# On VectorE, the sums of a vector panel put ahead of the split of the next weight panel

## The chip, the cores and the metric

The kernel runs on one core of one Trainium2 chip, as one launch. The metric is device time in microseconds. A core has TensorE (PE in the rows; its weight loads are PEld), VectorE (DVE), ScalarE (ACT), GpSimd (POOL) and SyncE (SP, which here only issues DMAs). Each engine works through its own instructions in order and waits on semaphores for the others.

## The reference, cut to what matters

Two blocks of two layers each are evaluated on 256 latent and 256 context tokens of width 1024, all in float32. The first block is a mixer (low-rank attention and neighbourhood attention behind gates) with an MLP, twice; the second is an mLSTM layer and a windowed attention layer. Every layer begins with a modulated norm whose shift, scale and gate come from a condition vector:

```
mod = silu(c) @ w_ada[layer] + b_ada[layer]          # (1024) @ (1024, 6 * 1024)
shift, scale, gate, ... = split(mod)                 # the vectors
x = x + gate * f(norm(x) * (1 + scale) + shift)
f: h @ w_in, gates, attention, w_out; relu(h @ w_ff1)**2 @ w_ff2
```

`c` is one vector for the latent tokens and another for the context tokens. So there are matrix products with 512 tokens, and matrix-vector products with one or two columns, and both read large weights from HBM.

## The kernel before, in words

All weights are read as 261 panels of at most 128 x 2048 floats (1 MB), in one list `items` that `plan()` writes. SyncE issues them in exactly that order into three buffers `raw[0..2]`, panel i into `raw[i % 3]`; it waits before each until panel i - 3 has been consumed. There are two kinds.

A weight panel is a 256-column piece of a matrix (8 chunks of 128 rows). To multiply in float32 accuracy it is split: ScalarE rounds it to `whi` (`hi`, L1236, two instructions of half a panel), VectorE subtracts to get the rest, `wlo` (`lo`, L1829, two halves). Then `raw` is free. `whi` and `wlo` have two buffers each, so `hi` of a panel also waits until TensorE is done with the panel two before it. TensorE multiplies hi x hi, hi x lo and lo x hi: 2 x 8 x 3 = 48 matmuls of 512 columns for a panel (L579 to L581 in `weight_left`), half of them for panels of 4 chunks (`mo`, `no`), and half the columns in layer 1, where only latent tokens count. It may start when the first half of `lo` is there (`weights`) and needs the other in mid panel (`rest`).

A vector panel ("ada") is 256 rows of a modulation matrix, 1024 columns. The first eight are multiplied on TensorE; the other 64 go to VectorE. `beside(p)` takes the vector panel that follows weight panel p in the list (the table `WITH`, built from `AFTER`) and adds c[k] * w[k] into `parts_of[0]` (latent) and `parts_of[1]` (context): four instructions of 128 x 1024 (L1824, in a vector's first panel two of them L1819), or two where only the latent part is needed (`LATENT_ONLY`). Four panels make one vector, q = 0 to 3. At q = 1 `beside` first reads the finished row of the vector before (`rows_out`). After the fourth, TensorE adds the partial sums up over the 128 partitions (`vector_sums`, L707), at the end of its panel p: there it waits for the sums (`("parts", r)`). ScalarE then copies the row (L1255) and TensorE turns it (L718) at the end of the next panel.

On VectorE the order is written by hand. `begin(p)` makes the `lo` of the weight panel after p, while TensorE works on p; `beside(p)` follows it; then comes what p's product needs: in the head loop (L2174 on) the branches of `mo` and `no`, in `wo` and `ff2` the residual and, in places, the sums of squares, in `ff1` the squared relu, in `mo` and `mz` of the mLSTM the output gates. Sixteen vectors ride this way: four in the head loop and `wo` of layer 0 (q = 3 falls on gm1, gn2, no3 and ff1's third panel), seven in the MLP of layer 0 (three of them full, r 7, 9 and 11, three for the latent part alone, and the one ahead of the turn to the next norm, full), one in `gn` of layer 1, one in `mq`, one in `mk`, two in `mo`.

```
def begin(p):                      # VectorE
    lo_to(next_weight(p))
# SyncE, per panel p of the list, q = items[p.i - 3]
wait used(q) if q is a vector panel else lo(q, 1);  dma_start(raw[p.slot], p)
```

Of the kernel before, what the change touches and what calls it, by code (L numbers as in the profile page):

```python
# [298 lines left out]
def program(nc, d, out):  # L299
    with ExitStack() as ctx:  # L300
# [131 lines left out]
        def S(n):  # L432
            return small[:, SMALL[n][0]:SMALL[n][1]]
# [6 lines left out]
        at = {p.key: p for p in items}  # L440
# [1366 lines left out]
        def vector(e):  # L1807
# [6 lines left out]
            def tt(o, a, b, op, *names):  # L1814
                e.tensor_tensor(o, a, b, op).then_inc(*up(ve, *names))  # L1815
# [7 lines left out]
            def stt(o, a, s_, b, o1, o2, *names):  # L1823
                e.scalar_tensor_tensor(o, a, s_, b, o1, o2).then_inc(*up(ve, *names))  # L1824
# [16 lines left out]
            def begin(p):  # L1841
                lo_to(next_weight(p))
# [204 lines left out]
            def first_layer(l):  # L2047
# [44 lines left out]
                for n, a in (("q", 1), ("k", 1)):  # L2092
                    p = at["na", l, 2 * "qk".index(n) + a]
                    begin(p)
                    beside(p)
                    tl = tiles if n == "q" else [0, 1, 2, 3]
                    if n == "k":
                        begin(at["uq", l, 0])
                    for tile in tl:
                        e.wait_ge(*done(("nsq", l, n, tile)))  # L2100
                        e.tensor_reduce(nss[n][:, 0, tile], work[:, tile, :].rearrange("p (h e) -> p h e", e=64), AX.X,
                                        ALU.add).then_inc(*up(ve, ("nsum", l, n, tile)))
                    if n == "q":
                        begin(at["na", l, 2])
                        beside(at["na", l, 2])
                    r = slice(tl[0], 4)
                    rsqrt_fine(nss[n][:, 1, r], nss[n][:, 0, r], nss[n][:, 2, r], 64, ("ns", l, n), ("nrt", l, n))
                    if n == "k":
                        begin(at["uq", l, 1])
                    for tile in tl:  # L2110
                        v = ntok(n, tile).rearrange("p c (h e) -> p c h e", e=64)
                        g_ = nss[n][:, 1, tile].rearrange("p (c h) -> p c h", h=2).unsqueeze(3).to_broadcast([128, 4, 2, 64])
                        tt(v, v, g_, ALU.mult, ("na normed", l, n, tile))
# [39 lines left out]
                a = tiles[0]  # L2153
                rsqrt_fine(mrms[:, 1], msums[:, 1], mscr[:, :, :], 96, ("ms", l, "k"), ("mrt", l, "k"))
                for tile in range(4):
                    w = ktok[:, tile]
                    tt(w, w, mrms[:, 1, tile].unsqueeze(2).to_broadcast([128, 8, 96]), ALU.mult, ("k normed", l, tile))
                rsqrt_fine(mrms[:, 0, a:4], msums[:, 0, a:4], mscr[:, a:4], 96, ("ms", l, "q"), ("mrt", l, "q"))
                begin(at["na", l, 4])
                beside(at["na", l, 4])  # L2160
                for n, dst in (("q", mqT), ("k", mkT)):
                    first = q0 if n == "q" else 0
                    for h in range(1, 8, 2):
# [9 lines left out]

                for h in range(4):  # L2174
                    for kind in ("gm", "gn", "mo"):
                        if h or kind != "gm":
                            begin(at[kind, l, h])
                        beside(at[kind, l, h])
                    for j in range(2):
                        key, u = ("mo", l, h, j), utmp[j][:, 0:nq]  # L2180
                        e.wait_ge(*done(("full", key)))
                        e.wait_ge(*done(("sig", l, "gm", h, j)))
                        tt(u, banks(key)[:, 0:nq], u, ALU.mult, ("read", key))
                    begin(at["no", l, h])
                    beside(at["no", l, h])
                    for j in range(2):
                        c = 2 * h + j
                        key, u = ("no", l, h, j), utmp2[j][:, 0:nq]
                        e.wait_ge(*done(("full", key)))
                        e.wait_ge(*done(("sig", l, "gn", h, j)))  # L2190
                        tt(u, banks(key)[:, 0:nq], u, ALU.mult, ("read", key))
                        own()
                        tt(u, u, utmp[j][:, 0:nq], ALU.add, ("ymix", l, c))
                        e.wait_ge(*done(("yhi", l, c)))
                        own()
                        tt(gYl[:, c, q0:T], u, gYh[:, c, q0:T].bitcast(F32), ALU.subtract, ("ylo", l, c))
# [7 lines left out]
                    return key if last else (*key, x)  # L2204

                for a in range(3):
                    begin(at["wo", l, a])
                    beside(at["wo", l, a])
                    for j in range(2):
                        residual(s, 2 * a + j, ("wo", l, 2 * a + j), "b", l, 2, parts)  # L2210
                        stat(s, 2 * a + j, parts)
# [7 lines left out]
                m = n = 0  # L2219
                for kind, g in MLP_ORDER:  # L2220
                    for a in range(4):
                        begin(at[f"ff{kind}", l, 4 * g + (1 if (kind, g, a, l) == (1, 0, 0, 0) else a)])
                        if kind == 2 and g == 3 and a == 3:
                            rows_out()
                            if not last:
                                fold("b", 1, 1, "gattn1")
                            turn(after, *(("s", 0, 1, 0) if last else ("b", 1, 1, 0)), parts,
                                 lambda j, x: residual(after, 6 + j, split_key(("ff2", l, 3, 6 + j), x), "b", l, 5, x),
                                 at["mq", 1] if last else at["ckv", 1, 1])
                            continue  # L2230
                        beside(at[f"ff{kind}", l, 4 * g + a])
                        for j in range(2):
                            c = 2 * a + j
                            if kind == 1:
                                u, v = utmp[m % 2][:, q0:T], utmp2[m % 2][:, q0:T]
                                e.wait_ge(*done(("relu", l, m)))
                                tt(v, u, u, ALU.mult, ("hsq", l, m))
                                e.wait_ge(*done(("hhi", l, m)))
                                own()
                                tt(H[g % 2][1][:, c, q0:T], v, H[g % 2][0][:, c, q0:T].bitcast(F32), ALU.subtract, ("hlo", l, g, c))  # L2240
                                m += 1
                            else:
                                residual(after, c, ("ff2", l, g, c), "b", l, 5, parts)
                                if g == 3:
                                    stat(after, c, parts)

                        if last:
                            if n == 1:
                                rows_out()
                                fold("s", 0, 1, "gnorm0")  # L2250
                            if n < 8:
                                stat("s0", n, "c")
                            elif n == EARLY:
                                rms("s0", "c")
                            elif n <= EARLY + 8:
                                scaled("s0", n - EARLY - 1, "c", "s", 0, 1)
                                left("s0", n - EARLY - 1, "c", "s", 0, 0)
                        n += 1

            def lstm_layer():  # L2260
# [10 lines left out]
                for o, m in ((tri[0], zb), (tri[1], zf)):  # L2271
                    ts(o[:, :], m[:, 384:512], -1.0, None, ALU.is_ge, None)
                for a in range(4):
                    if a:
                        begin(at["mq", a])
                    beside(at["mq", a])
                begin(at["mg", 0])
                key = ("mgT",)
                e.wait_ge(*done(("full", key)))
# [12 lines left out]
                for dr, order in ((0, (0, 1, 2, 3)), (1, (1, 0, 3, 2))):  # L2292
                    e.memset(pre[:, dr, order[0]], 0.0).then_inc(*up(ve))
                    for before, tile in zip(order, order[1:]):
                        own()
                        tt(pre[:, dr, tile], pre[:, dr, before], lf[:, before, dr, :], ALU.add, "gate pre")
                for a in range(4):
                    begin(at["mk", a])
                    beside(at["mk", a])
                    if a == 0:  # L2300
                        key = ("gsum",)
                        e.wait_ge(*done(("full", key)))
# [78 lines left out]
                mark(ve, "lstm dve end")  # L2381
                for g in range(2):
                    for a in range(4):
                        begin(at["mo", 4 * g + a])
                        beside(at["mo", 4 * g + a])
                        for j in range(2):
                            c = 8 * g + 2 * a + j
                            e.wait_ge(*done(("lsig", c)))
                            own()
                            stt(hnT[:, c, :], hnT[:, c, :], S("mlhg")[:, c:c + 1], s1[j][:, :], ALU.mult, ALU.mult)  # L2390
                        begin(at["mz", 4 * g + a])
                        beside(at["mz", 4 * g + a])
                        for j in range(2):
                            c = 8 * g + 2 * a + j
                            u = s1[2 + j][:, :]
# [226 lines left out]
```

## Time and profile before

| what | us |
|---|---|
| median of 3 runs | 2124.77 (2123.84 to 2125.97) |
| profiled execution | 2125.6 |
| its span, first to last instruction | 2123.8 |
| TensorE busy | 2002.0 (94%) |
| VectorE busy | 1374.1 (65%) |
| ScalarE busy | 908.7 (43%) |
| mean granted clock of TensorE | 0.976 |

The span is what the trace holds; the profiled execution's own time is 1.8 us more. Busy time is the time in which an engine has at least one instruction at work. The granted clock is 1.0 at TensorE's full rate of 2.4 GHz and 0.5 at 1.2 GHz.

### The profile page before, as it was taken

What the parts mean: (1) busy time and instruction counts of PE and PEld (TensorE: products, weight loads), DVE (VectorE), ACT (ScalarE), POOL (GpSimd) and SP (SyncE); (2) the same over time, 40 slices, a digit from 0 to 9 for tenths busy, and PEclk for the clock granted to TensorE, in tenths of its full rate; (3) what the DMA queues carried; (4) which work ended last, traced back from release to release, by engine and by line L of the source; (5) the groups of instructions that cost most, each with busy time, mean ns of one, the idle gap of its engine ahead of it and who ended that gap; (6) DMA issues with size and microseconds to landing.
All of it is one profiled execution on the core that took longest, in us unless ns stands there. A gap on an engine that the chain in (4) does not pass through costs nothing. (4 is left out here: it accounts for less than half of the span.)

```text
span 2123.8 us, 30218 instructions
## 1 busy us (share of the span) xinstructions
PE 2002.0 (94%) x12098; PEld 1674.8 (79%) x12098; DVE 1374.1 (65%) x2452; ACT 908.7 (43%) x1632; POOL 58.3 (3%) x83
## 2 busy tenths in 40 slices
PE   5999998988999999899999899998999999999998
PEld 3888776768787777698779899996787778888877
DVE  4447765668676766775676677665466665464886
ACT  4346752224422232255574465433243433233685
POOL 0000000001000000010000000000000000000100
PEclk9999999999999999999999899999999999999999
DMA  8222015443345454434107455534311133332311
GB/s 298 95 90 95 16 41 198 159 158 120 139 160 197 159 198 159 154 134 144 46 27 274 161 189 181 187 137 167 139 61 40 41 119 144 114 140 102 135 61 41
DMA packets 47099, 277.05 MB, mean 130 GB/s; under 512 B 4464, under 2 KB 12784, under 8 KB 16880
## 3 DMA queue, kind: packets, MB, share of 16 engines
q1 hardware_dynamic: 42080, 266.94, 34.1%
q10 hardware_dynamic: 4736, 7.34, 1.1%
q8 instruction: 96, 1.57, 0.3%
q0 software_dynamic: 144, 0.85, 0.1%
q14 instruction: 43, 0.35, 0.0%
HBM read 273.01 MB, written 2.10 MB: 130 GB/s over the span
## 5 line engine op out<-in xcount | busy, mean ns | idle before, releaser
L579 PE MATMUL ps<-t 128*128 128x512 f32 (+1 forms) x2176 | 761.8, 350 | 12.7 <-DVE t L1829 11.0
L580 PE MATMUL ps<-t 128*128 128x512 f32 (+1 forms) x2176 | 752.8, 346 | 0.0
L581 PE MATMUL ps<-t 128*128 128x512 f32 (+1 forms) x2176 | 752.5, 346 | 0.0
L1829 DVE TENSOR_TENSOR t<-t 128x1024 fp32r<-128x1024 f32 (+2 forms) x372 | 417.0, 1161 | 269.8 <-ACT t L1236 268.9
L1236 ACT ACTIVATE t<-t 128x1024 fp32r<-128x1024 f32 (+2 forms) x378 | 360.0, 1000 | 304.6 <-DMA t<-in_panels 188.7
L579 PEld LDWEIGHTS ps<-t 128*128 128x128 f32 x2176 | 416.3, 191 | 77.3 <-DVE t L1829 14.6
L580 PEld LDWEIGHTS ps<-t 128*128 128x128 f32 x2176 | 416.3, 191 | 50.7 <-issue 0.7
L581 PEld LDWEIGHTS ps<-t 128*128 128x128 f32 x2176 | 415.4, 191 | 51.5
L1824 DVE SCALAR_TENSOR_TENSOR t<-t 128x1024 f32<-128x1024 f32 (+7 forms) x415 | 332.6, 838 | 27.1 <-ACT t L1336 14.1
L1815 DVE TENSOR_TENSOR t<-t 128x512 f32<-128x512 f32 (+10 forms) x621 | 228.9, 389 | 154.1 <-ACT t L1273 41.7
L1336 ACT ACTIVATE t<-ps 128x512 f32<-128x512 f32 (+1 forms) x244 | 114.8, 491 | 244.0 <-PE ps L581 130.4
L660 PE MATMUL ps<-t 128*128 128x256 f32 (+1 forms) x524 | 158.9, 303 | 0.4 <-DVE t L1829 0.2
L662 PE MATMUL ps<-t 128*128 128x256 f32 (+1 forms) x524 | 152.2, 291 | 0.0
L661 PE MATMUL ps<-t 128*128 128x256 f32 (+1 forms) x524 | 152.2, 290 | 0.0
L1824 DVE SCALAR_TENSOR_TENSOR t<-ps,t 128x256 f32<-128x256 f32 (+2 forms) x176 | 83.2, 496 | 83.0 <-PE ps L581 59.2
L660 PEld LDWEIGHTS ps<-t 128*128 128x128 f32 x524 | 100.7, 192 | 9.4 <-issue 3.0
L661 PEld LDWEIGHTS ps<-t 128*128 128x128 f32 x524 | 100.8, 192 | 3.7 <-issue 2.2
L662 PEld LDWEIGHTS ps<-t 128*128 128x128 f32 x524 | 100.6, 192 | 1.4
L1815 DVE TENSOR_TENSOR t<-ps,t 128x128 fp32r<-128x128 f32 (+5 forms) x134 | 52.2, 394 | 63.1 <-ACT t L1704 31.5
L1359 ACT ACTIVATE t<-ps,t 128x512 f32<-128x512 f32 (+1 forms) x128 | 87.0, 696 | 10.2 <-DVE t L1815 10.2
L1273 ACT ACTIVATE t<-t 128x256 f32<-128x256 f32 (+1 forms) x62 | 30.9, 503 | 129.8 <-DVE t L1824 114.5
L1819 DVE TENSOR_SCALAR t<-t 128x512 f32<-128x512 f32 (+5 forms) x182 | 79.4, 477 | 2.5
(171 smaller groups left out, 2055.6 us busy)
## 6 DMA issues: line engine op xcount, KB each, us to landing
t<-in_panels SPq DMA_DIRECT2D x235, 1024.0 KB, 4.9
t<-in_panels SPq DMA_DIRECT2D x18, 512.0 KB, 4.0
t<-in_panels SPq DMA_DIRECT2D x8, 768.0 KB, 4.1
t<-in_window ACTq DMA_DIRECT2D x4, 768.0 KB, 4.3
t<-in_ctxT SPq DMA_DIRECT2D x1, 1024.0 KB, 13.4
t<-in_xT SPq DMA_DIRECT2D x1, 1024.0 KB, 15.5
t<-in_ctxT ACTq DMA_DIRECT2D x1, 1024.0 KB, 5.7
t<-in_xT ACTq DMA_DIRECT2D x1, 1024.0 KB, 5.6
```

The lines of the kernel that those rows point to most:

```text
L579: e.matmul(o, hi[:, k, w], xh[:, c0:c1], start=k == 0, stop=False)
L580: e.matmul(o, hi[:, k, w], xl[:, c0:c1], start=False, stop=False)
L581: t = e.matmul(o, lo[:, k, w], xh[:, c0:c1], start=False, stop=k == p.nk - 1)
L660: e.matmul(o, xh[:, r], hi[:, k, n0:n1], start=k == 0, stop=False)
L661: e.matmul(o, xh[:, r], lo[:, k, n0:n1], start=False, stop=False)
L662: t = e.matmul(o, xl[:, r], hi[:, k, n0:n1], start=False, stop=k == p.nk - 1)
L1236: e.activation(p.half(whi[p.buf], a), p.half(raw[p.slot], a), ACT.Copy).then_inc(*up(se, ("hi", p.i, a)))
L1336: e.activation(o, i, func, scale=scale).then_inc(*up(se, ("read", key), *names))
L1359: e.activation(work[:, 2 * par + g, x * w:x * w + w], banks(("s", s, i, g))[:, x * w:x * w + w], ACT.Exp, scale=sc_, bias=nm[:, c:c + 1], ...
L1815: e.tensor_tensor(o, a, b, op).then_inc(*up(ve, *names))
L1824: e.scalar_tensor_tensor(o, a, s_, b, o1, o2).then_inc(*up(ve, *names))
L1829: e.tensor_tensor(p.half(wlo[p.buf], a), p.half(raw[p.slot], a), p.half(whi[p.buf], a).bitcast(F32), ALU.subtract).then_inc(*up(ve, ("lo", ...
```

## The change

On VectorE `beside(p)` is called ahead of `begin(p)` in place of behind it, wherever both stand together. TensorE's, ScalarE's and SyncE's programs are the same text. In the MLP the call also moves ahead of the branch for the last panel, which has no vector panel. `beside` of the `na` and `mz` panels returns at once, as no vector panel follows them.

```diff
@@ the head loop of the first block
                 for h in range(4):
                     for kind in ("gm", "gn", "mo"):
+                        beside(at[kind, l, h])
                         if h or kind != "gm":
                             begin(at[kind, l, h])
-                        beside(at[kind, l, h])
...
+                    beside(at["no", l, h])
                     begin(at["no", l, h])
-                    beside(at["no", l, h])
...
                 for a in range(3):
+                    beside(at["wo", l, a])
                     begin(at["wo", l, a])
-                    beside(at["wo", l, a])
...
@@ the MLP
                     for a in range(4):
+                        beside(at[f"ff{kind}", l, 4 * g + a])
                         begin(at[f"ff{kind}", l, 4 * g + (1 if (kind, g, a, l) == (1, 0, 0, 0) else a)])
...
-                        beside(at[f"ff{kind}", l, 4 * g + a])
@@ the mLSTM layer
                 for a in range(4):
+                    beside(at["mq", a])
                     if a:
                         begin(at["mq", a])
-                    beside(at["mq", a])
...
                 for a in range(4):
+                    beside(at["mk", a])
                     begin(at["mk", a])
-                    beside(at["mk", a])
...
+                        beside(at["mo", 4 * g + a])
                         begin(at["mo", 4 * g + a])
-                        beside(at["mo", 4 * g + a])
...
+                        beside(at["mz", 4 * g + a])
                         begin(at["mz", 4 * g + a])
-                        beside(at["mz", 4 * g + a])
```

The same exchange stands at `na` 2 and `na` 4.

## Rows read from the trace of the kernel before

**Rows 1.** The waits of the whole span: engine, line, waited for: us, times, longest.
```profile
PE ps L707 <- DVE t L1824: 50.9, 10, 8.1
PE ps L579 <- DVE t L1829: 11.0, 12, 2.5
...
DVE t L1829 <- ACT t L1236: 268.9, 147, 15.1
...
ACT t L1236 <- DMA t<-in_panels: 188.7, 45, 11.2
...
ACT t L1236 <- PE ps L581: 76.1, 14, 9.5
```
**Rows 2.** TensorE's waits in stretches: 330-460, 540-560, 600-860, 885-900, 1110-1165, 1440-1530.
```profile
PE ps L707 <- DVE t L1824: 21.2, 3, 8.1
...
PE ps L707 <- DVE t L1824: 4.3, 1, 4.3
...
PE ps L707 <- DVE t L1824: 10.7, 3, 3.9
...
PE ps L707 <- DVE t L1824: 5.1, 1, 5.1
PE ps L718 <- ACT t L1255: 2.6, 1, 2.6
...
PE ps L579 <- DVE t L1829: 4.0, 6, 1.6
...
PE ps L707 <- DVE t L1824: 9.6, 2, 6.0
```
**Rows 3.** Timeline of the MLP: start, duration, engine, line, operation, [idle before <-releaser].
```profile
641.73 2.36 DVE L1829 TENSOR_TENSOR t<-t 128x1024 fp32r<-128x1024 f32 x2 [3.90 <-ACT t L1236]
644.00 4.87 DVE L1824 SCALAR_TENSOR_TENSOR t<-t 128x1024 f32<-128x1024 f32 x4
648.98 1.85 DVE L1824 SCALAR_TENSOR_TENSOR t<-ps,t 128x256 f32<-128x256 f32 x4
654.73 2.36 DVE L1829 TENSOR_TENSOR t<-t 128x1024 fp32r<-128x1024 f32 x2 [3.90 <-ACT t L1236]
...
648.90 0.80 SPq L539 DMA_DIRECT2D t<-in_panels  x2
...
653.64 2.01 ACT L1236 ACTIVATE t<-t 128x1024 fp32r<-128x1024 f32 x2 [2.35 <-DMA t<-in_panels]
```
**Rows 4.** A window: stretch, length, PE, PEld, DVE, ACT, POOL busy, clock, DMA, GB/s.
```profile
1721.40:1732.30 10.90, 10.90 (x49) 9.00 (x49) 9.18 (x11) 4.13 (x6) 0.00 (x0) 1.00 0.34 138
```
**Rows 5.** Windows of 14 us from the start of L707: the first and last of ten.
```profile
348.60:362.60 14.00, 13.96 (x67) 10.64 (x68) 5.01 (x6) 2.15 (x5) 0.00 (x0) 0.87 0.48 169
...
1516.60:1530.60 14.00, 14.00 (x75) 10.25 (x76) 3.85 (x10) 5.53 (x10) 0.00 (x0) 0.65 0.59 217
```
**Rows 6.** The sums: groups by form (busy, mean ns), and a multiplication pair in the timeline.
```profile
L1824 DVE SCALAR_TENSOR_TENSOR t<-t 128x1024 f32<-128x1024 f32 x189 | 232.7, 1280 | 0.7
...
850.01 1.41 DVE L1819 TENSOR_SCALAR t<-t 128x1024 f32<-128x1024 f32 x2
```
**Rows 7.** Timeline of the head loop and of the turn behind it, VectorE and TensorE.
```profile
335.26 0.68 DVE L1815 TENSOR_TENSOR t<-ps,t 128x512 f32<-128x512 f32 x1
...
340.09 0.69 DVE L1815 TENSOR_TENSOR t<-t 128x512 fp32r<-128x512 f32 x1 [0.70 <-ACT t L1561]
...
329.48 0.50 PE L579 MATMUL ps<-t 128*128 128x512 f32 x1 [2.36 <-DVE t L1829]
...
507.38 1.19 PE L728 MATMUL ps<-t 128*128 128x256 f32 x2 [5.70 <-DVE t L1815]
```
**Rows 8.** Timeline of VectorE in the last panels of wo.
```profile
491.47 4.87 DVE L1824 SCALAR_TENSOR_TENSOR t<-t 128x1024 f32<-128x1024 f32 x4
...
501.55 2.36 DVE L1829 TENSOR_TENSOR t<-t 128x1024 fp32r<-128x1024 f32 x2 [0.20 <-ACT t L1236]
```
**Rows 9.** Timeline of VectorE ahead of its work beside mo1.
```profile
1726.94 0.69 DVE L1815 TENSOR_TENSOR t<-t 128x512 fp32r<-128x512 f32 x1 [0.70 <-ACT t L1708]
```

More of the change, by code:

```diff
@@ L2103, in first_layer @@
                     if n == "q":
+                        beside(at["na", l, 2])
                         begin(at["na", l, 2])
-                        beside(at["na", l, 2])
                     r = slice(tl[0], 4)
@@ L2158, in first_layer @@
                 rsqrt_fine(mrms[:, 0, a:4], msums[:, 0, a:4], mscr[:, a:4], 96, ("ms", l, "q"), ("mrt", l, "q"))
+                beside(at["na", l, 4])
                 begin(at["na", l, 4])
-                beside(at["na", l, 4])
                 for n, dst in (("q", mqT), ("k", mkT)):
```

## The prediction, made before the kernel after was seen

> **What bounds the kernel now.** I read the busy table first: TensorE is busy for 2002.0 of 2123.8 us, VectorE for 1374.1, so the change can only pay through TensorE's idle time and through its clock. Then the waits of the whole span [rows 1]: the largest wait of TensorE is L707, the matmuls that add up a finished vector panel. It waits for VectorE's L1824 (the sums) 10 times, 50.9 us in all. L579 waits for L1829 (the low part of a weight panel, "lo" below) only 11.0 us. The same view shows VectorE waiting 268.9 us for ScalarE's L1236 (the high part, "hi"), and ScalarE 188.7 us for the panels' DMA. By stretch the 50.9 are 21.2 (three stalls in the head loop of layer 0), 4.3, 10.7 (three in the MLP), 5.1 and 9.6 (two in mq and mk) [rows 2].
>
> Why the sums are late stands in the timeline of one MLP group [rows 3]. lo starts at 641.73 and 654.73, every 13.0 us, while TensorE needs 10.9 us for a panel of 48 matmuls at the full clock [rows 4]. The 13.0 are a ring: lo 2.27 (641.73 to 644.00), the sums 4.87 (to 648.87), then SyncE issues the next weight panel at 648.90 into the slot that the sums gave back, ScalarE starts hi at 653.64, 4.74 later, and lo follows after its first half, 1.09 later. So the ring loses 2.1 us a panel, and TensorE pays at the fourth panel of a vector, where L707 waits (3.9 [rows 2]).
>
> The wait has a second price, the clock. In the 14 us from the start of L707 the granted clock is a mean of 0.87 in the first of them and 0.65 in the last (the first and the last of the ten, [rows 5]); between them stand 0.78, 0.85, 0.88, 0.88, 0.88, 0.89, 0.70 and 0.82. As it has the levels 1.2 and 2.4 GHz, (1 - clock) x 14 is the time lost: 1.8, 3.1 and 2.1 in the head loop, 1.7 at ff1, 1.7, 1.7 and 1.5 in the MLP, 4.2 ahead of the turn, 2.5 and 4.9 in mq and mk, together 25.2 us. The Trainium skill ("TensorE: Matmul & The Clock Gate", Terms) prices all half-rate time at half, the idle part too: by it the mean clock 0.976 costs the whole kernel 51 us. I count only stretches in which TensorE works, since half rate costs nothing to an engine that waits.
>
> **The change part by part.** No instruction is added or removed. On VectorE, "beside" moves ahead of "begin" (lo, 2.27). It is four instructions of 1.28, 4.87 from the first's start to the last's end; in a vector's first panel two of them are multiplications, 1.41 for the pair, together 3.8; a vector for the latent part alone has half, 2.6 or 2.0 [rows 6]. The hunks on "na" change nothing, as no vector panel rides with those keys. Three things follow.
> (1) The sums end earlier by a lo, 2.27, and by the wait for hi that stood before it (3.90 in rows 3).
> (2) SyncE, which issues strictly in the order of the list, issues the next weight panel that much earlier: its 4.74 now run beside lo, the residual and the next sums, and the ring of 13.0 is open. VectorE's own work for such a panel is 2.27 + 4.87 + 1.86 = 9.0, under the 10.9. The vector panel after it waits for lo's slot and is issued when it was before; it lands a panel ahead of its sums.
> (3) lo ends later by the sums, but only if hi was there. Say t is the start of a TensorE panel. Where VectorE comes to it at t + 3.6, as in the steady loops, lo's first half, all that TensorE needs to start, ends at t + 3.6 + 4.87 + 1.2 = t + 9.7: in time by 1.2. Come to later than t + 4.8, TensorE waits.
>
> Stretch by stretch, written out from the rows' durations:
> Head loop and output projection of layer 0 (330 to 508). The ceiling is 21.2 + 7.0 of clock = 28.2. Here VectorE is nearly the bound. After a "no" panel it has the four operations per half that join the branches, 5.5 us (335.26 to 340.8) [rows 7], so from the start of gm it needs 1.2 + 5.5 + 4.87 + 1.2 = 12.8 before gn may start: a new wait of 1.9, twice (gm2, gm3). The panel no is only 5.45 long: sums 4.87 and half a lo after the mo operations give new waits of 1.3 (h 1) and 0.3 (h 2). L707 after gm1 keeps 0.8. In wo residual and statistics take 5.0 between sums and lo (496.34 to 501.35, the 0.20 of hi left out [rows 8]), against 4.87 and a lo: 12.1 for a panel, and its three starts wait 0.7, 1.1 and 1.2. Sum 7.3; the wait of 2.36 for lo at 329.48 [rows 7] falls by 1.4, and of the 5.70 at 507.38 [rows 7] 1.2 go, as TensorE is less far ahead. 28.2 - 7.3 + 2.6 = 23.5; I take 22.5, as ScalarE's sigmoids stand in line with hi.
> ff1's third panel: 4.3 + 1.7. The sums come 2.6 earlier (lo and 0.3 of its wait), 1.7 stay: 4.3.
> MLP, three vectors: 10.7 + 4.9 = 15.6, all of it, as three of a vector's four panels are ff2 ones of 9.0, and the ff1 one has the short sums.
> Last vector before the turn: 5.1 and the 2.6 of L718 [rows 2], which waits for ScalarE's row copy behind two statistics. The sums come in time, the copy still does not: some 3.8 stay, and with clock 4.2 I take 6.
> gn of layer 1, at half the columns 5.5 a panel: sums of 2.6 or 2.0 and a short lo end in time, and the next gm's transfer is issued a short lo (1.2) earlier. The 4.0 of lo's waits in rows 2 go.
> mq and mk: 9.6 + 7.4 of clock = 17.0. Before each L707 TensorE has two panels of 10.9 or more since its last wait, and VectorE little but sums and lo, 7.1 a panel: all go.
> Gates mo and mz (1712 to 1912): no wait now, clock 1.00. VectorE comes to mo1 at 1727.6, 6.2 after TensorE's 1721.4 [rows 4, 9]: lo's first half at t + 12.3, a new wait of 1.4. Later ones are at t + 3.6: none.
> Sum: 22.5 + 4.3 + 15.6 + 6 + 4 + 17 - 1.4 = 68. Since some forty panels now have lo ready with about 1 us to spare, I give back 3 for those that miss by tenths: 65. The profiled execution took 2125.6; 2125.6 - 65 = 2060.6. The median of the runs is 0.8 lower: 2060.
>
> Bounds of what the trace does not show. The transfer that now shares the DMA engines with another: 4.74 [rows 3], twice that, 9.5, if it had half of them throughout. Issued at t + 6 it would land 4.6 into the next panel, with hi's half 1.1 later, and the sums, now first, end at 6: it costs 0. The Trainium skill ("DMA: Bandwidth & Descriptors", Bandwidth) gives 6.15 us for 1 MB: the old ring would be 14.4, the trace has 13.0. The new wait for lo: 0 to 1.9 a panel. The clock: 0 to 25.2 back.
>
> **The rivals.**
> A, only the order counts: the sums come 2.27 earlier, but hi is still held by something (the weight buffer that TensorE frees at t, or ScalarE's queue) and the lag rebuilds. For it: L1236 also waits 76.1 us for TensorE [rows 1]. Against: in rows 3 it is the DMA. Gain 10 x 2.27 = 23 and no clock, for stalls of over 2 us remain: 2102.
> B, slower: lo becomes the wait. Mechanism: the weights of the next panel stand behind 4.87 of sums in each panel, and where VectorE arrives after t + 4.8 the panel's start pays, each time, not once in four panels. If it arrives as late everywhere as behind gm, the 44 panels with sums for both token groups pay 1.9 each, 84 us, against the 68 gained: 2125.6 + 16 = 2141. For it: mo1 and gm2. Against: in the MLP VectorE waits 3.90 a panel in rows 3.
> C, no change: the sums, now first, wait for the vector panel's own DMA, and the ring only turns round; 2125. Against: that panel's slot is freed two panels before.
>
> **How the numbers follow.** Forecast 0.68 (2046 to 2078), A 0.2 (2078 to 2110), C 0.04, B 0.08. The ceiling, 50.9 + 25.2 + 4 = 80 off, is 2045. The range 2045 to 2088 leaves out C, B and part of A. What can be told from no change is about 0.2%, 4 us. Faster 0.9, same 0.03, slower 0.07.
>
> **What the profile would show.** Right: L707's wait for L1824 under 5 us with one or two places left, ScalarE's wait for the panels' DMA well under 188.7, lo in the MLP every 10.9 us, clock 1.00 behind 649, 745 and 841, and L579 waiting for L1829 some 10 to 15 us, in gn, no and wo. Wrong: lo still every 13 us (A), L579's wait for L1829 over 60 (B), or L1824 waiting for a DMA (C).

## The result, and the profile after

The changed kernel takes 2053.33 us (median of 4, 2053.07 to 2053.79) beside 2124.31 us of the kernel before (median of 4, 2122.58 to 2125.97): ratio 0.9666, interval 0.9649 to 0.9683. That is 71.0 us off; 2060 with 2045 to 2088 was forecast. The profiled span is 2051.2 us, 72.6 less than before.

The page of the kernel after: busy time of each engine, its share of the span and its instructions, and the granted clock in 40 slices.

```profile
span 2051.2 us, 30218 instructions
PE 1978.2 (96%) x12098; PEld 1659.7 (81%) x12098; DVE 1370.2 (67%) x2452; ACT 907.2 (44%) x1632; POOL 58.3 (3%) x83
...
PEclk9999999999999999999999999999999999999999
```

TensorE was busy for 2002.0 of 2123.8 us and is now busy for 1978.2 of 2051.2. Its matmuls are the same, so the 23.8 us of busy time that went are put down to the clock (mean 0.976 before, 0.993 now), and the other 48.8 of the 72.6 (121.8 idle before, 73.0 now) are waits. These are the two terms that the prediction added up.

The waits of TensorE after the change, as engine, line, waited for: us, times, longest:

```profile
PE ps L694 <- DMA t<-in_panels: 17.3, 5, 8.9
PE ps L579 <- DVE t L1829: 11.7, 13, 2.5
PE ps L624 <- DVE t L1824: 8.7, 3, 5.0
PE ps L728 <- DVE t L1815: 6.1, 3, 3.2
PE ps L600 <- DVE t L1824: 4.3, 1, 4.3
PE ps L718 <- ACT t L1255: 4.0, 3, 3.0
PE ps L579 <- DVE t L1815: 2.8, 3, 1.4
...
PE ps L707 <- DVE t L1824: 1.9, 2, 1.7
```

L707's 50.9 us for the sums [rows 1] have become 1.9, in two places. L579's wait for `lo`, which now stands behind the sums, went from 11.0 only to 11.7: old waits in `gn` of layer 1 left, new ones in the head loop came. What is at the top now are panels that TensorE multiplies alone at the start, which the change does not touch.

The waits of VectorE and ScalarE around the split, in the same columns:

```profile
DVE t L1829 <- ACT t L1236: 160.8, 96, 15.1
ACT t L1236 <- PE ps L581: 125.3, 23, 9.2
...
ACT t L1236 <- DMA t<-in_panels: 51.2, 14, 8.6
```

`hi` waited 188.7 us for the panels' transfers and 76.1 for TensorE [rows 1]; now 51.2 and 125.3. So most panels lie ready, and it is TensorE, giving back a weight buffer, that lets `hi` start. The MLP on VectorE, two panels of the group after 676 us (start, duration, operation):

```profile
677.03 4.87 DVE L1824 SCALAR_TENSOR_TENSOR t<-t 128x1024 f32<-128x1024 f32 x4
681.81 2.36 DVE L1829 TENSOR_TENSOR t<-t 128x1024 fp32r<-128x1024 f32 x2
...
691.24 2.36 DVE L1829 TENSOR_TENSOR t<-t 128x1024 fp32r<-128x1024 f32 x2
...
697.66 4.86 DVE L1824 SCALAR_TENSOR_TENSOR t<-t 128x1024 f32<-128x1024 f32 x4
702.44 2.36 DVE L1829 TENSOR_TENSOR t<-t 128x1024 fp32r<-128x1024 f32 x2
```

Neither the sums nor the low half waits for anything (there is no bracket behind them; in rows 3 it was 3.90 each time), and the low halves start 9.4 and 11.2 us apart, where they stood every 13.0. Over the twenty panels between the L707 at 571.70 and the one at 798.73 TensorE now takes 11.35 us a panel, the sums of the vectors with it; between the same instructions it took 12.06 (599.56 to 840.75). The clock behind two of the ten places (stretch, length, busy PE, PEld, DVE, ACT, POOL, clock, DMA share, GB/s):

```profile
617.20:631.20 14.00, 14.00 (x74) 10.94 (x74) 7.56 (x12) 3.72 (x5) 0.00 (x0) 1.00 0.48 187
...
1447.10:1461.10 14.00, 14.00 (x110) 12.06 (x110) 4.94 (x17) 6.42 (x12) 0.00 (x0) 1.00 0.23 76
```

All ten such windows have 1.00 now; before they went from 0.65 to 0.89 [rows 5].

New waits of TensorE behind `lo` in the head loop, as forecast, and one behind L1815, the end of the branches' work at the first panel of `wo`, which was not; then what is left ahead of the turns, at ff1's third panel and at L718:

```profile
364.97 0.50 PE L579 MATMUL ps<-t 128*128 128x512 f32 x1 [1.18 <-DVE t L1829]
...
377.46 0.50 PE L579 MATMUL ps<-t 128*128 128x512 f32 x1 [1.34 <-DVE t L1829]
...
413.63 0.50 PE L579 MATMUL ps<-t 128*128 128x512 f32 x1 [1.41 <-DVE t L1829]
...
443.67 0.50 PE L579 MATMUL ps<-t 128*128 128x512 f32 x1 [1.41 <-DVE t L1815]
...
483.40 1.19 PE L728 MATMUL ps<-t 128*128 128x256 f32 x2 [3.21 <-DVE t L1815]
...
526.65 1.07 PE L707 MATMUL ps<-t 128*32 128x256 f32 x16 [1.67 <-DVE t L1824]
...
848.85 0.41 PE L718 MATMUL ps<-t 128*128 128x128 f32 x2 [2.96 <-ACT t L1255]
```

Laid side by side at the same instructions, the two traces give the gain of each stretch:

| stretch | forecast | measured |
|---|---|---|
| head loop and `wo`, to the turn (L728 at 507.38 and 483.40) | 22.5 | 24.0 |
| ff1's third panel (L707 behind 599.56 and 571.70) | 4.3 | 3.9 |
| MLP, three full vectors (to the L707 at 893.31 and 844.81, its own wait left out) | 15.6 | 15.5 |
| last vector and the turn (to L624 at 914.72 and 863.99) | 6 | 7.3 |
| layer 1's `gn` (L707 at 1170.35 and 1115.35) | 4 | 4.3 |
| from there to layer 1's turn (TensorE's wait at L600, 1211.38 and 1154.32) | 0 | 2.1 |
| `mq` and `mk` | 17.0 | 17.0 |
| `mo` and `mz` | -1.4 | -1.5 |
| given back | -3 | 0 |
| sum, before rounding | 65 | 72.5 |

### The profile page after: what moved, and what is told of

The parts are those of the page before. It is cut to its first block and busy times, and to the rows that moved or that the text cites. A ratio compares the mean times of both kernels' runs of the same rounds, so it can differ in the third digit from the quotient of the medians.

```text
span 2051.2 us, 30218 instructions
## 1 busy us (share of the span) xinstructions
PE 1978.2 (96%) x12098; PEld 1659.7 (81%) x12098; DVE 1370.2 (67%) x2452; ACT 907.2 (44%) x1632; POOL 58.3 (3%) x83
## 5 line engine op out<-in xcount | busy, mean ns | idle before, releaser
L579 PE MATMUL ps<-t 128*128 128x512 f32 (+1 forms) x2176 | 756.3, 348 | 14.6 <-DVE t L1829 11.7
L581 PE MATMUL ps<-t 128*128 128x512 f32 (+1 forms) x2176 | 748.7, 344 | 0.0
L579 PEld LDWEIGHTS ps<-t 128*128 128x128 f32 x2176 | 412.3, 189 | 76.4 <-DVE t L1829 17.2
L1236 ACT ACTIVATE t<-t 128x1024 fp32r<-128x1024 f32 (+2 forms) x378 | 359.8, 1000 | 216.3 <-PE ps L581 125.3
L581 PEld LDWEIGHTS ps<-t 128*128 128x128 f32 x2176 | 412.1, 189 | 50.8
L1815 DVE TENSOR_TENSOR t<-t 128x512 f32<-128x512 f32 (+10 forms) x621 | 228.8, 389 | 163.3 <-ACT t L1273 42.3
L1815 DVE TENSOR_TENSOR t<-ps,t 128x128 fp32r<-128x128 f32 (+5 forms) x134 | 52.2, 394 | 63.9 <-ACT t L1704 33.5
## 6 DMA issues: line engine op xcount, KB each, us to landing
t<-in_xT SPq DMA_DIRECT2D x1, 1024.0 KB, 15.6
```

What stands on the lines that cost most here:

```text
L579: e.matmul(o, hi[:, k, w], xh[:, c0:c1], start=k == 0, stop=False)
L581: t = e.matmul(o, lo[:, k, w], xh[:, c0:c1], start=False, stop=k == p.nk - 1)
L1236: e.activation(p.half(whi[p.buf], a), p.half(raw[p.slot], a), ACT.Copy).then_inc(*up(se, ("hi", p.i, a)))
```

## The experiments

In what follows "the theory" is the prediction's: a ring of low half, sums, transfer and high half, 13.0 us against TensorE's 10.9, which the new order opens; the clock comes back with it.

### Each part alone

The first three kernels are the kernel before with one region in the new order (only the added lines are shown; the same call behind `begin` is taken out in each):

```diff
@@ MLP only
+                        beside(at[f"ff{kind}", l, 4 * g + a])
                         begin(at[f"ff{kind}", l, ...
@@ head loop, no and wo only (both layers)
+                        beside(at[kind, l, h])
                         if h or kind != "gm":
                             begin(at[kind, l, h])
@@ mq and mk only
+                    beside(at["mk", a])
                     begin(at["mk", a])
```

MLP only:

> Only the MLP's hunk of the change (sums ahead of lo for the vector panels that ride with ff1 and ff2 of layer 0). Theory (an open ring, and the clock): in the two traces the distance between before and after grows in this stretch by 2.3 + 1.5 at ff1's third panel, 15.5 over the three full vectors and 7.3 ahead of and in the turn, 26.6 in all: 2124.3 - 26.6 = 2097.7. Rival A (only the order counts, 2.27 for each of five stalls, 11): 2113.

Measured: 2097.75 us, ratio 0.9884 (0.9858 to 0.9910).

Head loop, `no` and `wo` only:

> Only the hunks of the head loop (gm, gn, mo, no, both layers) and of wo. Theory: 24.0 by the turn of layer 0 and 4.3 + 1.8 in and behind gn of layer 1, as the two traces stand apart: 2124.3 - 30.1 = 2094. Rival A (three stalls at 2.27, 7): 2117. Rival B (lo becomes the wait, no gain here since VectorE is nearly the bound): 2124 or more.

Measured: 2096.71 us, ratio 0.9872 (0.9848 to 0.9895).

`mq` and `mk` only:

> Only the hunks of mq and mk. Theory: both stalls go and the clock with them, 9.6 + 7.4 = 17.0: 2107. Rival A (two stalls at 2.27, 4.5): 2120.

Measured: 2106.54 us, ratio 0.9920 (0.9899 to 0.9942).

Against 2125.63 of the kernel before beside them the parts bring 27.9, 28.9 and 19.1, together 75.9, and with the 1.5 lost in `mo` 74.4, against 71.0 for the whole change. Each is within 3 us of its expectation, and 13 to 20 us from rival A (only the order by 2.27 counts). The parts are nearly independent: they add up to within 3.4 us.

### The ring opened without the new order

The kernel before, in its old order, but in the MLP the vector panels have `raw[2]` for themselves, the weight panels share the other two, and SyncE issues each weight panel ahead of the vector panel:

```diff
+        if first <= p.i < end:                 # ff1 (0, 2) to ff2 (0, 15)
+            p.slot = 2 if p.whole else w % 2
+            w += not p.whole
...
+        if out[i] is items[i] and items[i].whole and not items[i + 1].whole:
+            out[i], out[i + 1] = out[i + 1], out[i]
...
-                if p.i >= NRAW:
-                    q = items[p.i - NRAW]
+                if p.prior is not None:        # the slot's last panel
+                    q = p.prior
```

> VectorE's order as in the kernel before (lo, then sums). In the MLP of layer 0 alone, the three buffers are split by kind: vector panels in one, weight panels in the other two, and SyncE issues a weight panel ahead of the vector panel that stood before it; so a weight panel's transfer no longer waits for the sums just before its own lo. Theory (the ring of lo, sums, transfer, hi is what makes the sums late): VectorE's 9.0 us a panel fit into 10.9, the MLP's three waits of 10.7, the one of 5.1 and their clock go although the order is the old one, 20 us or more: 2104 or less, and lo stands every 10.9 us. Rival A (the order on VectorE is what counts): no gain, 2124, and lo still every 13.0 us.

Measured: 2109.20 us, ratio 0.9929 (0.9914 to 0.9944). VectorE in this kernel (its L1852 is `lo`, L1847 the sums), and L730 (the L707 of before):

```profile
634.48 2.36 DVE L1852 TENSOR_TENSOR t<-t 128x1024 fp32r<-128x1024 f32 x2 [0.28 <-ACT t L1259]
636.76 4.87 DVE L1847 SCALAR_TENSOR_TENSOR t<-t 128x1024 f32<-128x1024 f32 x4
...
644.42 1.07 PE L730 MATMUL ps<-t 128*32 128x256 f32 x16
...
646.92 2.36 DVE L1852 TENSOR_TENSOR t<-t 128x1024 fp32r<-128x1024 f32 x2 [1.51 <-ACT t L1259]
```

The low half still stands ahead of the sums, and L730 waits for nothing. From 602.33 to 704.51 nine steps of the low half take 11.35 us each. From the L707 behind ff1's third panel (598.92) to that of the last full group (825.95) are 227.03 us; in the changed kernel they are 227.03 as well (571.70 to 798.73), in the kernel before 241.2 (599.56 to 840.75). So here the order itself is worth nothing: the ring was the whole loss. The kernel's time is 5 above the bound of 2104: in the last vector ahead of the turn L730 still waits 3.12, and from there to the next wait (875.23 to 897.00) the granted clock is 0.84.

With both, the slots and the new order:

> The same split of the buffers in the MLP, with the changed order. Theory: the ring is open in either, so it adds nothing to the change: 2053 +- 2. Rival A: gains that are independent add up, 2033.

Measured: 2052.02 us, ratio 0.9668 (0.9651 to 0.9686). Once open, it is open: the gains are one and the same and do not add.

The same slots and issue order outside the MLP, from gm0 of layer 0 to wo2 and from mq1 to mk3, again with the old order on VectorE:

> The order of before everywhere, but from gm0 of layer 0 to wo2, and from mq1 to mk3, the vector panels have a raw slot of their own, the weight panels share the other two, and SyncE issues each weight panel ahead of the vector panel. This opens the ring without the new order. Theory: in mq and mk the 17.0 us gained there are the ring alone, and all of them come back (15 to 17). In the head loop VectorE stands close behind TensorE, so the low half ahead of the sums still makes L707 wait 2 to 3 us at q3 of most vectors; of the 24.0 gained there some 14 to 18 come back. Sum 2124.5 - 32 = 2092 (2089 to 2096). Rival, the order itself counts at every vector (L707 waits at q3 whatever the slots): half or less, 2107 or more. Rival, all of it is the ring: 41 gained, 2083.

Measured: 2105.03 us, ratio 0.9909 (0.9894 to 0.9924). 20 us, not 32: the theory's range is missed by 9 us, and the time is nearer to the rival in which the order counts at every vector (2107 or more). In the trace 11 are gained by the end of `wo`, where 14 to 18 were expected, and between the panels at 1426.45 and 1550.14 of the kernel before, with `mq` and `mk` in between, 7.6, where 15 to 17 were. VectorE in `mq` (L1851 the sums, L1856 `lo`, SPq SyncE's issues, L734 the L707 of before):

```profile
1430.70 1.28 DVE L1856 TENSOR_TENSOR t<-t 128x512 fp32r<-128x512 f32 x2
...
1430.81 1.53 SPq L566 DMA_DIRECT2D t<-in_panels  x3
...
1435.80 4.87 DVE L1851 SCALAR_TENSOR_TENSOR t<-t 128x1024 f32<-128x1024 f32 x4 [3.81 <-DMA t<-in_panels]
...
1440.82 1.07 PE L734 MATMUL ps<-t 128*32 128x256 f32 x16 [1.95 <-DVE t L1851]
```

Now the sums wait for their own panel: with one slot it is issued only when the sums before it end (1430.81) and lands 5.0 us later. 4.87 and 5.0 are a second ring, of 9.9 us, which leaves VectorE little to gain on TensorE. That this ring is the whole of the shortfall is argued, not shown: the same slots cost nothing in the MLP. So outside the MLP no run separates slots and order; this one shows that more slots for one kind of panel is not what the new order does.

### Is it the earlier transfer?

ScalarE's wait for transfers fell from 188.7 to 51.2. Whether that is a cause or a by-product, these two runs tell: the changed kernel, with SyncE held back to issue a weight panel only when TensorE is done with the panel whose weight buffer it will take. In the MLP:

```diff
                         e.wait_ge(*done(("lo", q.i, 1)))
+                    if p.key in MLP_PANELS[4:31]:
+                        e.wait_ge(*done(("used", p.before.i)))
```

> The changed kernel, but SyncE issues a weight panel of the MLP only when TensorE has used the panel whose buffer it will take, so its transfer no longer starts under the work ahead. Theory (the new order takes the transfer out of the ring by laying the sums beside it): the transfer of 4.7 us lies beside the sums of 4.87 us, the low half starts within 1 us of where it did, and TensorE has that much slack: 2053.3, within 3 us. Rival (the gain in the MLP is that the weight panels now arrive earlier): the 15.5 us of the MLP go, with the clock, to 2069 or more.

Measured: 2051.88 us, ratio 0.9659 (0.9645 to 0.9673). ScalarE's waits for transfers (L1238 is its L1236) in this kernel:

```profile
ACT t L1238 <- DMA t<-in_panels: 159.0, 35, 11.5
```

159.0 us, of 188.7 in the kernel before, and the time does not move; 569.90 to 796.93 is again 227.03. In the MLP the early issue is a by-product. What counts is that the transfer lies beside the sums in place of behind them.

Everywhere:

```diff
+                if p.before is not None and items[p.i - 1].whole and items[p.i - 2].key in WITH and not p.on_pool():
+                    e.wait_ge(*done(("used", p.before.i)))
```

> The changed kernel, but SyncE issues every weight panel that stands behind a vector panel, in the head loop, the MLP, layer 1 and the last block, only when TensorE has used the panel whose buffer it will take. Theory (with the sums first the transfer always lies beside the sums): where the panel is used for 10.9 us or more nothing changes; in the head loop, where TensorE already waits 1.2 to 1.4 us for the split at four places, those waits may grow by up to the 4.7 of the transfer less the 4.87 of the sums, so little: 2053.3 to 2058. Rival (outside the MLP the gain rests on the panel having arrived earlier, since there opening the ring by slots gave back only 20 of 41 us): part of the head loop's 24.0 and of the 17.0 in mq and mk goes, 2065 or more.

Measured: 2066.53 us, ratio 0.9726 (0.9705 to 0.9747). 13.2 us more than the changed kernel, above the theory's range (to 2058) and in the rival's (2065 or more), by 1.5: the theory's forecast failed here. TensorE where most of it goes (L581 is L579 of before), and SyncE's issue and ScalarE's `hi` ahead of it:

```profile
1374.40 1.40 SPq L541 DMA_DIRECT2D t<-in_panels  x3
...
1379.29 2.00 ACT L1238 ACTIVATE t<-t 128x1024 fp32r<-128x1024 f32 x2 [13.05 <-DMA t<-in_panels]
...
1381.70 0.77 PE L581 MATMUL ps<-t 128*128 128x512 f32 x1 [7.38 <-DVE t L1831]
```

At the entry to the last block nothing stands beside the transfer: it is issued at 1374.40, `hi` starts at 1379.29, and TensorE waits 7.38 where it waited 2.54. With what surrounds it this one place costs 7.5 of the 13.2 (1120.63 to 1405.73 is 285.10, it was 277.60). The head loop and `wo` lose 3.8 of the 24.0 gained there, at starts of panels behind the short panels `no`, as here:

```profile
403.88 0.50 PE L581 MATMUL ps<-t 128*128 128x512 f32 x1 [1.44 <-DVE t L1831]
...
441.90 0.50 PE L581 MATMUL ps<-t 128*128 128x512 f32 x1 [1.91 <-DVE t L1831]
```

The changed kernel does not wait for `lo` at these two places; at the third, `gm` of h 2, it waits 1.18 and this one 1.65. Some 1.5 more are clock at the turn, and all behind 1405.73, the rest of `mq`, `mk` and both vectors of `mo`, loses nothing (443.77 to the L707 at 1849.50, it was 443.81). So in the MLP, `mq`, `mk` and `mo` the rival is out; early issue is worth something where one kind of work begins and behind the short panels of the head loop.

### The clock by itself

Before the wait of L707, TensorE multiplies ones by ones in the bank that it is about to write, as many times as roughly fills the wait; the waits stay, the idleness goes:

```diff
                 o = bank(key, (7,))
+                for _ in range({2: 28, 3: 16, 4: 28, 5: 14, 7: 13, 9: 11, 11: 12, 12: 18, 14: 22, 15: 12}.get(r, 0)):
+                    e.matmul(o[:, 0:128], ones[:, :], ones[:, :], start=True, stop=True)
                 e.wait_ge(*done(("parts", r)))
```

> The kernel before, with 128x128 matmuls of ones by ones put ahead of the wait of L707 (11 to 28 of them, 2.3 to 6.0 us, always less than the stall that stood there); their result is overwritten by the sums that follow. No order is changed; TensorE is kept at work in the stall. This measures the clock alone. Theory as predicted (the clock is a price of its own that adds to the stalls): the 25.2 us of half-rate time mostly come back, 2124.3 - 22 = 2102. Rival (absorbed: where VectorE's ring sets the pace, a TensorE that works faster only waits longer at the next L707): 2116 to 2124, with L707's waits as long or longer than 50.9 when the filler's time is added.

Measured: 2111.34 us, ratio 0.9944 (0.9922 to 0.9966): 14.3 us off, between the theory's 2102 and the rival's 2116. The windows of 14 us behind two of the three places in the MLP:

```profile
640.10:654.10 14.00, 13.98 (x67) 10.87 (x67) 6.93 (x10) 2.39 (x3) 0.00 (x0) 0.88 0.47 170
735.70:749.70 14.00, 13.95 (x73) 10.90 (x74) 7.81 (x12) 2.39 (x3) 0.00 (x0) 1.00 0.59 213
```

Six of the ten windows have 1.00. But between the same instructions of the MLP the kernel is no faster: 589.62 to 831.25 is 241.6, before 241.2. The group behind 735.75, at the full clock, takes 45.3 where it took 46.9, and the next takes 50.2 in place of 49.1. TensorE comes sooner to an appointment that the ring sets. Of the 15.4 by which this trace is shorter than that of before, 3.0 stand already ahead of the first edited place, at 329.48 of before, and 1.9 come in layer 1 between 1170.35 and 1426.45, where nothing was edited either; 5.5 come in the head loop and `wo`, 3.7 in `mq` and `mk`. So in this trace 4.9 of the 15.4 are not the edit's. The clock's loss is no addend of its own as long as another ring is the bound; it becomes one when the ring is opened.

### A half-way order

In the changed kernel TensorE waits at several panels for the first half of `lo`, which now stands behind 4.87 us of sums. This kernel makes that half ahead of the sums and the second behind them:

```diff
+            def half(p):
+                i = next_weight(p)
+                if p.key in WITH and i < len(items) and nxt[0] <= i and not items[i].on_pool():
+                    lo(items[i], 0)
+                    half_done.add(i)
...
+                        half(at[kind, l, h])
                         beside(at[kind, l, h])
                         if h or kind != "gm":
                             begin(at[kind, l, h])
```

> The changed order, but the first half of lo stands ahead of the sums and the second half behind them. Theory: TensorE starts a panel on the first half of lo alone, so the new waits of the change (1.18, 1.34, 1.41 and 1.41 in the head loop, 1.28 at mo1, some in wo) go, and L707 waits at most 1.2 longer where it waits at all (ff1's third panel, 1.67): about 5 us, 2048. Rival: VectorE now waits for hi ahead of the sums again, the ring closes in part: 2056 to 2070.

Measured: 2078.86 us, ratio 0.9787 (0.9772 to 0.9801), worse than either theory. Its waits:

```profile
DVE t L1829 <- ACT t L1236: 223.6, 147, 15.1
...
ACT t L1236 <- DMA t<-in_panels: 162.5, 32, 10.1
```
```profile
PE ps L579 <- DVE t L1829: 15.7, 17, 2.5
PE ps L707 <- DVE t L1824: 11.1, 5, 3.6
```

The half ahead of the sums puts the wait for `hi`, and so the transfer, back in line with them: by the durations of rows 3 the ring is then transfer 4.74, `hi` 1.09, half a `lo` 1.2 and the sums 4.87, 11.9 us. That is over the 10.9 by half as much as before, and the trace shows it in the MLP, where first halves of `lo` start 11.9 us apart:

```profile
613.92 1.23 DVE L1829 TENSOR_TENSOR t<-t 128x1024 fp32r<-128x1024 f32 x1 [2.76 <-ACT t L1236]
...
625.86 1.23 DVE L1829 TENSOR_TENSOR t<-t 128x1024 fp32r<-128x1024 f32 x1 [2.83 <-ACT t L1236]
```

L707 waits again for over 3 us in three places (3.31 at 348.18 is the first), and even the wait for `lo` that the edit was to remove has grown to 15.7. The MLP's time is unharmed, 227.03 once more: over the three panels between a vector's start and its L707 the lag is now some 3 us, and before, of 3 x 2.1 = 6.3, TensorE waited for 3.3 to 3.9 only. So 2.4 to 3.0 were to spare, by this estimate about as much as the new lag.

Only at the nine places where TensorE waits for `lo`:

```diff
+                if p.key in SPLIT and ...   # no0-no2, gm2, gm3, wo0-wo2 of layer 0, mo1
```

> The changed kernel with the low half's first half ahead of the sums at nine places alone, where TensorE waits for the split in the changed kernel (no0 to no2, gm2, gm3 and wo0 to wo2 of layer 0, mo1). Theory (the ring closes only by repetition, and a single early half shortens the wait behind the sums): the waits of 1.18, 1.34, 1.41, 1.4 and 1.28 us shrink by half to all, 2048 to 2050. Rival (each early half puts 1.1 us between the panel's arrival and the sums, and that comes back at L707, as in the run with it everywhere): 2053 to 2060.

Measured: 2054.43 us, ratio 0.9668 (0.9652 to 0.9684), no better than 2053.33 and in the rival's range. The waits for `lo` fall from 11.7 to 9.9, L707 takes back 1.6 (3.5 in place of 1.9) and L728 1.5 (7.6 in place of 6.1).

### The one loop that lost

```diff
@@ changed kernel, mo and mz back
-                        beside(at["mo", 4 * g + a])
                         begin(at["mo", 4 * g + a])
+                        beside(at["mo", 4 * g + a])
```

> The changed kernel with the loop of mo and mz back in the order of before; the rest changed. Theory: the 1.5 us by which this loop was behind come back: 2051.8. Rival: the 1.28 us wait at mo1 was taken out of slack that returns elsewhere: 2053.3, no change. Either is small beside the interval of the comparison; the trace of this loop tells them apart.

Measured: 2052.19 us, ratio 0.9660 (0.9645 to 0.9674). The medians can't tell it from 2053.33. The loop itself can: from the last wait of L1093 to the L707 in `mo` (1617.48 to 1705.20) are 87.7 us, in the changed kernel 89.1 (1614.26 to 1703.39), before 87.7. So the 1.28 of mo1 is real and local, and this version is the better by 1.4, within the noise of the whole.

## Why the prediction was right

- **The ring** [rows 3]. Right, and isolated in the MLP alone. Own slots in the MLP open it in the old order and give the new order's time to the hundredth (227.03), and holding the transfers back there under the new order costs nothing. In the head loop, `mq` and `mk` the gain came as forecast, but the run that was to give it without the new order gave half, so how much of it is ring and how much order stays open. One reading of point (2) was too strong: that the next transfer starts earlier is not what pays; that the sums no longer stand between slot and transfer is.
- **VectorE's 9.0 per panel is under 10.9; lo is in time by 1.2.** Right in the MLP, `mq` and `mk`: no wait for `lo` there but the 2.54 at mq0, which stood there before. In the MLP there was more to spare than 1.2: TensorE starts the panels behind the `lo` of 681.81 and 691.24 at 685.46 and 696.66, and their first halves of 1.22 are ready 2.4 and 4.2 us earlier. The transfers that share the DMA engines cost nothing, as bounded. For a panel of 1 MB the trace has 4.74 [rows 3], and 5.0 at 1430.81 above, both from the issue to the start of the engine that waited for it. The Trainium skill ("DMA: Bandwidth & Descriptors", Bandwidth) gives 6.15 for 1 MB, measured on transfers that GpSimd issues; SyncE issues these, and the measured 4.74 decides.
- **The new waits.** Forecast and measured: those of 1.9 at the start of gn, h 2 and 3, measured 1.34 (377.46) and 1.41 (413.63); that of 1.3 behind no of h 1, measured 1.18 (364.97); ff1's third panel 1.7, measured 1.67; L718 3.8, measured 2.96; the turn 4.5, measured 3.21; mo1 1.4, measured 1.28. All are a little short. L707 after gm1, forecast 0.8, is 0.27 at 340.11.

  The sum of the head loop is another matter. The 0.3 behind no of h 2 and the three in `wo` (0.7, 1.1 and 1.2) are not there as waits for `lo`; the one wait in `wo` is the 1.41 at 443.67. The prediction's sum of these has a slip: 1.9 twice, 1.3, 0.3, 0.8, 0.7, 1.1 and 1.2 are 9.2, and it has 7.3. By its own terms the head loop would have given 21.6, not 23.5, before the 1.0 taken off. The new waits measured come to 5.6. From 327.12 to 507.38, and between the same instructions after, from 327.57 to 483.40, TensorE's idle time went from 29.2 to 10.0 us and its busy time from 151.0 to 145.9, 5.2 of clock where 7.0 stood in the sum. So 24.0 against 22.5 is three misses, waits too high, their sum too low and the clock too high, that largely cancel, and that part is luck.
- **The clock.** 23.8 us of busy time came back; of the 25.2 counted at the ten places, 23 were in the sum. So counting only stretches in which TensorE works was the right size. Within the span the time at half rate went from 102.5 to 30.7 us (the part of it in which TensorE was busy from 74.8 to 22.5). The rule of the Trainium skill ("TensorE: Matmul & The Clock Gate", Terms) takes half of all of it, which makes an estimate of 35.9 us; the measured 23.8 is less.
- **The give-back of 3** was the term sized wrong: no panel of the MLP, `mq` or `mk` missed, with 2.4 and 4.2 us to spare where about 1 was assumed. It and the head loop's 1.5 are most of the 6.7 between 2060 and 2053.3. Two smaller ones: the 2.1 ahead of layer 1's turn, for which I had nothing, and the turn of the MLP, 7.3 for 6. Both are in part luck of the clock. The MLP's stretch from L718 to L624 took 16.91 before and 15.14 after (the last section shows why). Of the 2.1, 1.4 come between 1181.30 and 1206.08: 24.78 us at a granted clock of 0.92 before, 23.35 at 1.00 after (1126.04 to 1149.39). The run with fill work, which edits nothing there, has 23.35 at 1.00 too (1171.43 to 1194.78), and the one with `mq` and `mk` alone 24.80 at 0.93 (1181.10 to 1205.90).
- **Rival A** fell with the first three runs, and with the MLP's own slots. **Rival B**'s mechanism is there, behind gm and no and at mo1, but it stays at 1.2 to 1.4 a time and in four places. **C** fell with the result: no sums wait for their panel's transfer in steady loops; the run with one slot for vector panels shows what that looks like (3.81).

## What to carry to other kernels

When two streams of panels share a few buffers and one in-order issuer, write the cycle out as a sum of durations (consume, free, transfer, convert, consume) and compare it with the bound engine's step; put the work that needs no new transfer first, so that it covers the one that does. A half-measure that puts any wait for the transfer ahead of that work closes the cycle again. A stall that shows at every fourth panel can be the toll of a small excess in each.

## What the runs showed of the hardware

The clock granted after the same stall is not the same in each execution. Ahead of the turn the changed kernel and the one with `mo` back run the same instructions and wait the same 2.96 us at L718; the windows from there to the next wait, first of the one, then of the other:

```profile
848.85:863.99 15.14, 12.23 (x100) 12.00 (x101) 7.78 (x14) 4.24 (x10) 0.02 (x1) 1.00 0.19 70
```
```profile
848.80:866.59 17.79, 14.88 (x100) 14.65 (x101) 7.78 (x14) 4.23 (x10) 0.02 (x1) 0.83 0.17 61
```

Clock 1.00 against 0.83, 2.65 us on one stretch of 15. Differences of two or three microseconds between two traces at one place behind a stall need this look before they are given a cause. The Trainium skill ("TensorE: Matmul & The Clock Gate", Part 1) says of a kernel's start that the number of slow matmuls differs between runs of one kernel; these two windows show such a difference in mid kernel.

And a clock regained need not be time regained: with fill work the time at half rate fell from 102.5 to 51.2 us, the kernel gained 14.3, some of it outside the edited places, and in the MLP nothing.
